# First projections in two-part precision, side projections merged, roots by logarithm, and two gate units moved, in a two-block network kernel

## The reference

```python
h = jnp.concatenate([meta, x], axis=1)            # 16 meta tokens + 256 = 272
n = _rmsnorm(h, pre_mix_norm)
proj = n @ w_in                                   # gq gk gv gz gb ga aq ak av iq ik iw gates
# first mixer
qkv = jax.nn.silu(_causal_conv(concat[gq, gk, gv], conv_w))   # 4 taps over tokens
q = _l2norm(q) * 128 ** -0.5; k = _l2norm(k)      # per head, x * rsqrt(sum(x*x) + eps)
beta = sigmoid(gb); g = -exp(a_log) * softplus(ga + dt_bias)
o = _gated_delta_rule(q, k, v, beta, g)           # chunks, triangular inverses
# second block
a = softmax(q1 k1) - lam * softmax(q2 k2)         # 8 heads, 512 keys
attn = rmsnorm(a @ v, subln_g) * (1 - lam_init)
y = sigmoid(ga) * (attn @ w_ao) + sigmoid(gf) * (four @ w_fo)
x = x + g1 * (y @ w_o)
# then 16 experts of which each token takes two, and a last norm
```

## Time and profile before

| what | value |
|---|---|
| median of 3 runs | 1325.09 us (1316.67 to 1333.52) |
| the profiled execution's own time | 1316.48 us |
| its span | 1314.7 us |
| mean granted TensorE clock | 0.967 of full speed |
| DMA moved | 254.60 MB, 194 GB/s on average |

### The profile page before, as it was taken

How to read it: one execution, slowest core, us unless ns; L and a number is a source line. 1 busy time by engine, 2 the same in 40 slices (tenths; PEclk the granted TensorE clock), 3 DMA queues, 4 the chain that set the end, 5 groups by cost and what they waited for, 6 DMA issues and landing times.

```text
span 1314.7 us, 21492 instructions
## 1 busy us (share of the span) xinstructions
PE 1232.9 (94%) x9008; PEld 1048.1 (80%) x9008; DVE 703.1 (53%) x1218; ACT 483.5 (37%) x768; POOL 29.3 (2%) x38
## 2 busy tenths in 40 slices
PE   7999878999999989999998999897899899999997
PEld 6886768998888969999997889665899766666655
DVE  4689576567866556664546333677555532112223
ACT  2176232363446444554344312465233201011112
POOL 0000012100000000000000000000001000000000
PEclk9998988999999998999998999899899899999999
DMA  9334211054341565554554422201557959999990
GB/s 367 128 128 178 111 67 62 1 173 163 122 153 65 215 235 193 186 177 177 178 184 158 177 78 97 97 1 79 210 180 273 379 225 419 420 420 420 420 397 32
DMA packets 36012, 254.60 MB, mean 194 GB/s; under 512 B 4016, under 2 KB 4160, under 8 KB 5584
## 3 DMA queue, kind: packets, MB, share of 16 engines
q1 hardware_dynamic: 33696, 238.88, 47.4%
q0 software_dynamic: 2224, 14.37, 2.8%
HBM read 252.19 MB, written 1.05 MB: 193 GB/s over the span
## 4 chain that ended last, share of the span: by engine, by line
PE 83%; DVE 12%; ACT 2%; issue 2%; DMA 0%; DVEq 0%; ACTq 0%
PE bank L1185 13%; PE bank L628 10%; PE bank L622 10%; PE bank L623 10%; PE bank L584 8%; PE bank L595 5%; PE bank L975 5%; PE bank L1024 3%; PE bank L982 2%; PE bank L660 2%; PE bank L1203 1%; PE bank L746 1%; PE bank L641 1%; DVE q L2275 1%; PE bank L761 1%
## 5 line engine op out<-in xcount | busy, mean ns | idle before, releaser
L1777 DVE TENSOR_TENSOR ring_low<-ring,w_high 128x2048 fp32r<-128x2048 f32 x93 | 212.7, 2289 | 164.0 <-ACT w_high L1367 163.8
L1367 ACT ACTIVATE w_high<-ring 128x2048 fp32r<-128x2048 f32 x93 | 178.5, 1919 | 320.9 <-PE bank L628 228.2
L595 PE MATMUL bank<-nT,ring 128*128 128x272 f32 x384 | 89.1, 393 | 3.2 <-DVE nT L1790 3.2
L595 PEld LDWEIGHTS bank<-nT,ring 128*128 128x128 f32 x384 | 72.9, 190 | 18.9 <-issue 4.0
L1185 PE MATMUL bank<-more,xs 128*64 128x256 f32 x704 | 84.3, 379 | 1.4 <-DVE xs L2427 1.4
L622 PE MATMUL bank<-hcl,w_high 128*128 128x256 f32 (+1 forms) x288 | 82.1, 316 | 2.3 <-DVE hcl L2229 2.2
L623 PE MATMUL bank<-hcl,w_high 128*128 128x256 f32 (+1 forms) x288 | 79.4, 307 | 0.0
L1185 PEld LDWEIGHTS bank<-more,xs 128*64 128x64 f32 x704 | 54.6, 137 | 27.4 <-issue 2.3
L622 PE MATMUL bank<-nT_high,w_high 128*128 128x256 f32 (+1 forms) x272 | 67.4, 290 | 0.0
L622 PE MATMUL bank<-nMs,w_high 128*128 128x256 f32 x256 | 65.1, 292 | 2.0 <-DVE nMs L2174 2.0
L623 PE MATMUL bank<-nMs,w_high 128*128 128x256 f32 x256 | 64.8, 291 | 0.0
(11 more groups left out here) (522 smaller groups left out, 2530.8 us busy)
## 6 DMA issues: line engine op xcount, KB each, us to landing
ring<-stream SPq DMA_DIRECT2D x168, 1024.0 KB, 5.0
more<-stream SPq DMA_DIRECT2D x56, 1024.0 KB, 16.3
more<-stream POOLq DMA_DIRECT2D x10, 1024.0 KB, 14.5
c<-constants_one SPq DMA_DIRECT2D x1, 1653.0 KB, 17.0
qc<-h_in SPq DMA_DIRECT2D x4, 272.0 KB, 4.3
c<-constants_two POOLq DMA_DIRECT2D x1, 1056.0 KB, 10.3
hT<-h_in POOLq DMA_DIRECT2D x1, 1024.0 KB, 6.1
ctxT<-ctx_in POOLq DMA_DIRECT2D x1, 1024.0 KB, 6.1
```

What stands on the lines that cost most here:

```text
L595: last = nc.tensor.matmul(dst[:, 0:n], w[:, k, j * 128:(j + 1) * 128], rhs[:, k, :], start=(k == 0), stop=(k == KT - 1))
L1367: A(w_high[:, d % 2, :], ring[:, s, :], ACT.Copy).then_inc(high_ready, 1)
L1777: TT(ring_low[:, s, :], ring[:, s, :], w_high[:, d % 2, :], sub).then_inc(low_ready, 1)
```

## The change

The first unit stays plain and the other eleven become split units, for which `nT_high` and `nT_rest` (high and low part of `nT`) are made at the start. q comes before v. ScalarE makes the first tap of 20 of the 24 tiles, GpSimd the product by the sigmoid. The sums for the norms are copied out to `sums`, and at the end all roots are made by Ln and Exp with scale -0.5, without a reciprocal. The weights of `av`, `gba` and `iw` are loaded beside each other by GpSimd's queue, and TensorE makes the three in one pass of 280 columns for each of three token tiles; `av` leaves the ring. In the second attention `gate2a` 0 goes into the first step, `gate2a` 1 behind the last, and the roots of the heads' norm are made by Ln and Exp. Key tiles of the first attention are cut as 16, 128, 128.

```diff
-    order = [("gk", u) ...] + [("gv", u) ...] + [("gq", u) ...]
-    order += [("mod", u) for u in range(6)] + [("av", 0)] + [("mod", u) for u in range(6, 8)]
+    order = [("gk", u) ...] + [("gq", u) ...] + [("gv", u) ...]
+    order += [("mod", u) for u in range(8)]
...
+        if half == 0:
+            order += [("gate2a", 0), ("gate2a", 1), ("mod", 18), ("mod", 19), ("ao", 0), ("ao", 1)]
...
@@ tensor
+                    split_tiles(kind, u, lambda k: nT_high[:, k, :], lambda k: nT_rest[:, k, :], T, names)
                 for i in range(12):
-                    if L2_AFTER[i] in (t - 4, t - 3):
+                    if L2_READS[i] in (t - 4, t - 3):
                         l2_sum(i)
-            (gba, later iw and av: groups of their own)
+            pe.wait_ge(beside_loaded, 48)
+            for g, (a, m) in enumerate(AV_TILES):
+                dst = take(("avgba", g), 2)
+                done(("avgba", g), group(dst[0:m, 0:UNIT_COLS + 24], [(nT[:, k, a:a + m], beside[:, k, :]) for k in range(KT)]))
...
                 if n + 1 < len(ATT):
                     scores2(n + 1)
+                if n == 0:
+                    split_tiles("gate2a", 0, lat(0), lat(1), SEQ, [("gate2a", 0)])
...
+            split_tiles("gate2a", 1, lat(0), lat(1), SEQ, [("gate2a", 1)])
             pe.wait_ge(sq_ready, 15)
@@ gpsimd
-            pool.dma_start(ws[:, :], ws_in).then_inc(ws_loaded, 16)
+            pool.wait_ge(nT_ready, KT)
+            (four dma_start: av, gba, iw into beside; ik)
+            for t in range(24):
+                pool.wait_ge(sig_ready, t + 2)
+                nc.gpsimd.tensor_tensor(conv_dst(t), conv_dst(t), scr[:, t % 2, 0:T], mul).then_inc(conv_ready, 1)
@@ scalar
+            for k in range(KT):
+                act.wait_ge(nT_ready, k + 1)
+                A(nT_high[:, k, :], nT[:, k, :], ACT.Copy).then_inc(nT_high_ready, 1)
+            highs(1)
...
+            for u in range(CONV_UNITS):
+                t = 2 * u
+                for j in range(2):
+                    if t + j < DVE_TAPS:
+                        tap(t + j)
+                if t >= DVE_TAPS:
+                    continue
+                sigmoid(t)
+                highs(min(u + 2, CONV_SPLIT))
+                sigmoid(t + 1)
+                (squares of tiles t-2, t-1; sums of t-4, t-3 copied out)
+            l2_roots()
+            for t in range(DVE_TAPS, 24):
+                sigmoid(t)
...
-                    A(nT_high[:, :, :], nT[:, :, :], ACT.Copy).then_inc(nT_high_ready, 1)
...
+                if n == 2:
+                    evac(("gate2a", 0), gate2[:, 0, :], 512)
+                    after_unit("gate2a", 0)
...
-                rms_root(("hss", j), 512, ...)
+                step(A(q2[...], full(act, ("hss", j))[:, :], ACT.Ln, bias=eps, scale=1.0 / 128))
+            step.settle()
+            for j in range(4):
+                A(q2[...], q2[...], ACT.Exp, scale=-0.5).then_inc(free(("hss", j)), 1)
@@ vector
+                TT(nT_rest[:, k, :], nT[:, k, :], nT_high[:, k, :], sub).then_inc(nT_rest_ready, 1)
+            lows(1)
...
-                step(TS(dst, bank[:, 0:T], sm[:, a + 3:a + 4], None, mul))
+                if t < DVE_TAPS:
+                    dve.wait_ge(tap_ready, t + 1)
...
-                if t >= 1:
-                    silu(t - 1)
-                (l2_norm: reciprocal and product)
+                if t % 2 == 1:
+                    lows(min(t // 2 + 2, CONV_SPLIT))
...
+                if n == 2:
+                    after_unit("gate2a", 0)
...
-                step(nc.vector.reciprocal(r, r))
```

More of the change, by code:

```diff
@@ L82, in weight_order @@
     for half in range(2):
-        for u in (2 * half, 2 * half + 1):
-            order += [("gate2a", u)] + ([("mod", 18), ("mod", 19)] if u == 0 else []) + [("ao", u)]
+        if half == 0:
+            order += [("gate2a", 0), ("gate2a", 1), ("mod", 18), ("mod", 19), ("ao", 0), ("ao", 1)]
+        else:
+            for u in (2, 3):
+                order += [("gate2a", u), ("ao", u)]
         order += [("gate2f", 2 * half), ("gate2f", 2 * half + 1), ("fo", half)]
@@ L221, in build @@
             with ExitStack() as same:
+                nT_rest = sbr(same, "nT_rest", 128, KT, T)
+            with ExitStack() as same:
                 low = sb(same, "low", 128, NSYS, 128)
@@ L233, in build @@
                 qc = sb(m, "qc", 128, H, T)
+                with ExitStack() as same:
+                    sums = sb(same, "sums", 128, H * T + 4 * 512)
+                    beside = sb(same, "beside", 128, KT, UNIT_COLS + 24)
                 v_beta = sb(m, "v_beta", 128, NSYS, 128)
@@ L542, in key_tiles @@
             n = nkeys(qt)
-            return [(a, min(128, n - a)) for a in range(0, n, 128)]
+            return [(0, META)] + [(a, 128) for a in range(META, n, 128)]
         ATT = [(qt, h) for qt in range(2) for h in range(H)]
@@ L1277, in _ @@
                     sp.dma_start(ring[:, s, :], stream[i * SLOTS + s]).then_inc(unit_loaded[s], 16)
+            for s in range(REST):
+                sp.wait_ge(unit_used[s], BASE)
+                sp.dma_start(ring[:, s, :], stream[BASE * SLOTS + s]).then_inc(unit_loaded[s], 16)
             s_last, n_last = ring_unit(ORDER.index(("wo2", 3)))
@@ L1401, in _, with tap, sigmoid @@
-            for t in range(24):
+                A(dst if i < H else dst.rearrange("p (a b) -> p a b", b=SEQ), src, ACT.Square).then_inc(sq_ready, 1)
+            def tap(t):
                 kind, j = CONV_TILES[t]
-                emptied(act, (kind, j))
+                A(conv_dst(t), full(act, (kind, j))[:, 0:T], ACT.Copy, scale=sm[:, tap_at(t, 0):tap_at(t, 0) + 1]).then_inc(tap_ready, 1)
+            def sigmoid(t):
+                emptied(act, CONV_TILES[t])
                 if t >= 2:
-                    act.wait_ge(silu_ready, t)
+                    act.wait_ge(conv_ready, t - 1)
@@ L1417, in _ @@
-            l2_root(10)
-            l2_root(11)
+                    emptied(act, ("l2", i))
+                for a, b in ((0, H * T), (H * T, H * T + 4 * 512)):
+                    step(A(sums[:, a:b], sums[:, a:b], ACT.Ln, bias=eps))
+                step.settle()
+                for j in range(4):
+                    A(sums[:, 2 * j * T:2 * (j + 1) * T], sums[:, 2 * j * T:2 * (j + 1) * T], ACT.Exp, scale=-0.5).then_inc(l2_ready, 1)
+                for j in range(4):
+                    A(l2_sums_of(H + j), l2_sums_of(H + j), ACT.Exp, scale=-0.5).then_inc(l2_ready, 1)
@@ L1674, in _ @@
             for j in range(4):
-                rms_root(("hss", j), 512, q2[:, 2 * j:2 * j + 2, :].rearrange("p a b -> p (a b)"), 128)
+                step(A(q2[:, 2 * j:2 * j + 2, :].rearrange("p a b -> p (a b)"), full(act, ("hss", j))[:, :], ACT.Ln, bias=eps, scale=1.0 / 128))
+            step.settle()
+            for j in range(4):
+                A(q2[:, 2 * j:2 * j + 2, :], q2[:, 2 * j:2 * j + 2, :], ACT.Exp, scale=-0.5).then_inc(free(("hss", j)), 1)
+            after_unit("gate2a", 1)
             for half in range(2):
@@ L2060, in _ @@
             turn(8)
-            emptied(dve, "iw")
+            for g in range(2):
+                emptied(dve, ("avgba", g))
             for n, (qt, h) in enumerate(ATT):
```

218 lines of the change are left out of this document (110 added, 108 removed).

## The result

The changed kernel took 1280.85 us in the median of five runs (1278.92 to 1298.43), the kernel before 1324.72 us beside it (1316.67 to 1333.52, five runs). The ratio is 0.968 with a 95% interval of 0.963 to 0.973: 3.2% faster. The forecast was 1288.7 us, its range 1272 to 1306. From median to median the gain is 43.9 us, where 36.4 us were forecast.

The account below looks back on a forecast made before the run. VectorE was taken to bound the convolution's 84 to 118 us, with TensorE waiting for the heads' norm in the second attention. Gains of 27.3 + 9.1 = 36.4 us took 1325.1 to 1288.7 us, range 1272 to 1306.

Parts of the forecast that it names:

- own-profile sum: Whole kernel: the profiled execution's 1316.5 us less 36.4 us gives 1280.1 us; that profile lay 8.6 us under the median.
- First place: Convolution and side projections up to L723: by TensorE's own work it begins at 115.8 instead of 143.10 us, gaining 27.3 us.
- GpSimd's product: Convolution's product by the sigmoid at 272 columns: 0.67 us, bounds 0.41 and 1.10; meeting VectorE's low part costed at nothing.
- Do the others keep up?: Convolution, each split unit: TensorE needs 6.9 us, VectorE 5.4 and ScalarE 5.3, so TensorE sets the pace.
- round of 6.2 us: Convolution: three taps, sigmoid, high part and low part handed between VectorE and ScalarE, 0.7 us shorter than TensorE's 6.9 us.
- rival A: Convolution: VectorE and ScalarE's round becomes the bound at 7.9 us, 13.8 us lost, 1302.5 us; chance 0.17 shared with another rival.
- rival B: Convolution: TensorE's small pauses for high parts cost it its clock; at half clock 73.1 us more, 1362 us; chance 0.04.
- thinnest cover: Ahead of L723: roots, sigmoids, betas, decays and copies end at 114 us, 2 us ahead of TensorE's 115.8 us.
- rival E: Heads' norm: Ln and Exp share one table load, so 1.28 us between them are not spent; 1287.4 us, chance 0.03.
- Second place: Second attention to the end of `ao` 1: it ends at 934.0 instead of 943.1 us, gaining 9.1 us.
- the low part in step 2: Second attention: VectorE waits for a high part and makes a low part, delaying by 3.3 us, bounds 0 and 4.2.
- Rival C: Second attention: delay over 4.2 us in step 2 and later sums cancel the gain there; 1297.8 us, chance 0.08.

Follow-up runs that it names:

- all_dve: The changed kernel with the convolution's first taps and its products by the sigmoid both back on VectorE: 1281.87 us, ratio 0.970 to the kernel before.
- product_dve: The changed kernel with only the product by the sigmoid moved from GpSimd back to VectorE: undisturbed 1281.4 us, ratio 0.978 to the kernel before with all four runs.
- low_later: The changed kernel with the preparation (high and low part) behind `gate2a` 0 moved from step 2 to behind the second attention's last step: 1275.62 us, ratio 0.962.
- low_later_again: The same kernel as `low_later`, run once more beside `both_behind` on one chip: 1273.66 us, ratio 0.965 to the kernel before.
- both_behind: `low_later` with `gate2a` 0 made behind the second attention's last step and `gate2a` 1 behind the sums of the heads' norm: 1277.85 us, ratio 0.971.
- heads_recip: The changed kernel with the heads' norm by Sqrt and VectorE's reciprocal, gate units left as in the change: 1291.85 us, ratio 0.978 to the kernel before.
- second_only: The kernel before with only the second attention's part of the change: 1311.16 us, ratio 0.991 to the kernel before.
- unmerged: The changed kernel with `av`, `gba` and `iw` as three passes rather than one of 280 columns: 1291.83 us, ratio 0.978 to the kernel before.

## Why the prediction was right, point by point

**The own-profile sum was right, 1280.1 us against 1278.07 us; the term that was mis-sized is the 8.6 us added to it.** I took the median of three runs of before as 8.6 us above its profiled execution and carried that over to the change. The runs of before scatter by themselves, from 1314 to 1328 us in most, and the profiled one lies near their lower end: its medians stay 4.5 to 8.2 us above it. The change scatters less: its median was 1280.85 to 1281.62 us, that is 3 us above its good profile. Of the error of 7.9 us, 5.8 are this term (8.6 less 2.8) and 2.0 the sum. So in the medians the change won some 5 us more than in the profiles, which no term of mine had. Where they lie was not traced; the slower runs of before show a lower mean clock (0.960 at 1324.84 us, 0.968 at 1316.34 us).

**First place: right in the sum, 115.78 us for 115.8, by errors that cancel, so that the agreement to 0.02 us is luck.** Split units came 6.93 and 6.87 us apart where 6.9 was forecast, and the merged pass took 11.32 us for 11.4. The start was 0.6 us shorter, the first unit 9.26 us long instead of 7.33 (its clock was 0.76), and the six `mod` units 5.32 us instead of 6.8. That last figure was read the earlier trace rows where the granted clock was low (0.79 between 118 and 125 us of before), and now it is 1.00: it was no property of the work.

**Terms of the 27.3 us.** By taking one away: splitting 12.6 us in the median (forecast 14.6), merging 10 us in the median (16.3 in the trace, with a lower clock), the roots by logarithm 22 to 24 us, and nothing each for GpSimd's product and ScalarE's taps. They don't add up to 27.3 since they overlap: the logarithm's worth is what the new order would have to pay otherwise.

**Do the others keep up?** Yes, but not for my reason. I reasoned from a round of 6.2 us with 0.7 us to spare, and saw rival A as the next likely; nor did I have VectorE's overlap. `all_dve` puts 1.9 us more on VectorE for each unit and loses nothing over these ten units. So my reading now is that with a unit in hand between the engines a round of handovers isn't what counts; the busiest engine's own sum is, with its overlap. TensorE's clock held at 1.00 and rival B never showed.

**GpSimd's product: wrong size, no effect.** Forecast 0.67 us, bounds 0.41 and 1.10. Measured (GpSimd of the changed kernel, in order of time):

```profile
84.12 0.78 POOL L1345 TENSOR_TENSOR vc<-vc,scr 128x272 f32<-128x272 f32 x1 [2.18 <-ACT scr L1445]
86.25 2.57 POOL L1345 TENSOR_TENSOR vc<-vc,scr 128x272 f32<-128x272 f32 x1 [1.36 <-ACT scr L1445]
```

0.78 us by itself, and 2.57 us where it meets the low part (85.89 us, 2.29 us long on VectorE). VectorE's low part stayed at 2289 ns in the mean, as before; it never began while GpSimd was in a product. At the end VectorE's products of q did, and there each held up the other (first GpSimd, then VectorE):

```profile
99.57 4.91 POOL L1345 TENSOR_TENSOR vc<-vc,scr 128x272 f32<-128x272 f32 x4 [10.74 <-ACT scr L1445]
...
101.45 4.18 DVE L1899 SCALAR_TENSOR_TENSOR qc<-qc,sums 128x512 f32<-128x512 f32 x4
```

GpSimd's four took 1.2 us each rather than 0.78, and VectorE's four 4.18 us, where they take 2.49 us in `product_dve`, whose GpSimd does nothing then. The Trainium skill, "SBUF — State Buffer", section "SBUF: two separate sides", has the two exclude each other, whichever starts first. The trace agrees on both sides: GpSimd waited out the low part, and both waited in the last products.

**The thinnest cover held by 1.0 us, not 2.** The roots ended at 97.7 us (forecast 99), sigmoids at 102.7 us (102), but VectorE's products of q only at 105.6 us: four took 4.18 us while GpSimd was at its last four. The last copy ahead of L744 ended at 114.8 us.

**Ln and Exp need a load each, as forecast;** rival E is gone. ScalarE of the changed kernel:

```profile
88.05 4.02 ACT L1452 ACTIVATE sums<-sums,eps 128x2176 f32<-128x2176 f32 x2
92.08 1.28 ACT L1455 ACT_TABLE_LOAD   x1
93.38 2.30 ACT L1455 ACTIVATE sums<-sums 128x544 f32<-128x544 f32 x4
```

**Second place: gain 8.7 us for 9.1.** The term for the low part in step 2 was 3.3 us with bounds 0 and 4.2. The steps from first to last transposes grew from 51.2 to 56.5 us, 5.3 us, of which `low_later` gets all back and 1.5 us more. So it was mis-sized by 2 us and lay out of its bounds. The high and low part were right by their bound, 4.1 us in the chain; what I left out is that TensorE waits longer than before by it and comes out of the pause at 1.2 GHz: 0.45 us more for the transposes, 0.8 and 0.95 us for the eight and four matmuls behind them than in `low_later_again`. `both_behind` bounds what the idea is worth: with `gate2a` 0 in the pause and the low part in the steps the place takes 127.3 us, without either 124.0, with the pause filled and the low part outside 120.6 us. As the change does it, filling the pause costs 3.3 us against `both_behind`. Done as in `low_later_again` it is worth 3.4 us: 1.4 in the steps, which no longer begin at 1.2 GHz, and 2.0 behind them, where `both_behind` has the high part ahead of the Ln. Another order on ScalarE might win those 2.0 us back without the pause; that was not run. The whole of the second place's gain is the reciprocal that went: `heads_recip` costs 10 us in the median and 11.3 us in the place. Rival C, that the place gives nothing, is gone with `second_only`.

**Rest.** The stretch between the places kept its length to about 1 us, which was the step I feared most. Behind the second place 1.3 us were gained that no term had (332.3 to 331.0 us); what they are was not tried.

**What stays open:** where the kernel before loses the time by which its median lies above its profile, and what sets the clock of the first unit, which moves L744 by up to 4 us. The new cut of the key tiles and the copy that went were not tried by themselves; that they are worth nothing rests on the stage between the places, which kept its length within what it varies by.

## What to carry to other kernels

When work is moved into one engine's pause, price what it makes the other engines do afterwards: `gate2a` 0 was free for TensorE, but the preparation behind it put 4.1 us of ScalarE and VectorE into the chain two steps later, and moving only the preparation out made the place 6.8 us shorter and the median 7 to 8 us. An engine that is busy 95% of a stretch is not a bound as long as its sum, taken from start to start and not from durations, stays at the pace of the leader and it has a unit in hand; before relieving it, put the work back and look. Carry the forecast against the profiled execution, and don't add the distance of one profile to a median of three.

## What the hardware showed

- Sixteen matmuls of 272 columns, three times over (high by high, high by rest, low by high), cost 6.0 us where the plain unit of 32 instructions costs 7.33 us.
- A GpSimd product of 272 columns takes 0.78 us alone and 2.57 us when it begins 0.36 us into a two-input instruction of VectorE of 2.29 us, which is not slowed. When products of both alternate, both are: VectorE's four products of q took 4.18 us beside GpSimd and 2.49 us without.
- Records of VectorE instructions overlap by about 0.07 us where the next doesn't wait for the last, 0.4 us in a unit's 7.3 (`all_dve`).
- The same first unit took 7.57 to 10.63 us by the clock granted at the start (1.00 down to 0.53 between 14 and 21 us), so that L744 moved by up to 4 us between profiles that are the same up to there.
- f32 instructions of 8 columns still cost TensorE 0.11 us each at a granted clock of 1.00 (before, 32 in 3.50 us from start to start, 128.97 to 132.47 us); the 96 of 16 and 8 columns in `unmerged` 0.14 us each at 0.84.
- Behind the 144 instructions of that pass the granted clock was 0.52 (119 to 125 us) though TensorE had no pause; behind the merged 48 it was 1.00.
